# Query weights of the latents: two loads of four heads in place of eight loads of one head

## The chip, the core and the metric

The kernel runs on one core of a Trainium2 chip. The metric is the device time of one execution in microseconds, lower is better. Before the change three runs gave 2002.58, 1998.96 and 2002.11 us, so the median is 2002.11 us. The profiled execution is a run of its own: it took 2000.01 us, of which 1998.2 us are the span from the first to the last instruction.

## The reference, cut to what matters

One layer of a network: a token mixer (state space scan, short convolution, output projection) and then a retrieval stage called PEER. There are 128 context tokens and 512 latent tokens of 1024 values, all float32. The change touches the queries of PEER alone:

```python
PEER_HEADS, PEER_NKEYS, PEER_TOPK, PEER_DQ, TOKEN_BLOCK = 8, 128, 16, 256, 128

def peer(h, w_query, sub_keys, expert_u, expert_v):
    def block(xb):                                   # 128 tokens
        q = (xb @ w_query).reshape(TOKEN_BLOCK, PEER_HEADS, 2, PEER_DQ // 2)
        s = jnp.einsum("thse,sne->thsn", q, sk)
        s1, i1 = lax.top_k(s[:, :, 0], PEER_TOPK)
        s2, i2 = lax.top_k(s[:, :, 1], PEER_TOPK)
        ...
        top, pos = lax.top_k(cand, PEER_TOPK)        # 16 experts for each token and head
        hid = jnp.einsum("thkd,td->thk", expert_u[idx], xb)
        act = gelu(hid) * softmax(top)
        return jnp.einsum("thk,thkd->td", act, expert_v[idx])
```

`w_query` is 1024 x 2048, that is 8 MB; one head's part is 1 MB. Five blocks of 128 tokens with eight heads and sixteen experts make 640 gathers of 128 rows, each row 8 KB (a row of expert_u and one of expert_v side by side).

## The kernel before, in words

The first 230 us or so do the modulation, the scan and the context's mixer. From then on the kernel is one long loop on all engines over G = 0 to 39 (`NALL`), one G for each block of 128 tokens and head: G 0 to 7 are the context's heads, G 8 to 39 those of the four latent blocks. In each G there are eight steps g (`NPR`), and each takes two experts k of the sixteen.

- GpSimd (POOL) issues the gathers, one an expert, into eight slots of 1 MB (`rows`, L1851). Gather k waits until TensorE has used the slot's last content (`v_done`).
- VectorE (DVE) multiplies the gathered rows with the tokens (`dot`, L1654), scales the result (`weigh`, L1663 and L1666), and does in between the top-k of head G+1 (L1595 to L1640).
- ScalarE (ACT) applies the gelu (L1211) and copies scores out of PSUM.
- TensorE (PE) adds the weighted rows (`add_rows`, L841), which frees two slots at each g. It also computes the query of head u = G+2. For the context (u under 8) this is small (L776). For the latents (u = 8 to 15, so G 6 to 13) it is done for all 512 latent tokens at once: `query_lat(u, 0)` stands ahead of `add_rows` at g = 4 and `query_lat(u, 1)` ahead of it at g = 5, 32 matmuls of 128x512 in all (L809), and then come the scores (`scores_lat`, L818) at g = 6. The text calls these 16 us "the block of u". TensorE runs its instructions in order, so in the block `add_rows` comes late, and with it the freeing of slots.
- Beside this, in G 0 to 6, the latents go through their own mixer (`latent_front`): the last output tiles of TensorE (L922, counted by `zol_mm`) are done in G 5, and VectorE normalises the latents (L1737, L1741) in G 6, after which ScalarE modulates them (L1067). Only then can the block of u = 8 start.

SyncE (SP) issues all plain loads, in program order, each behind its wait. There is one place for a head's query weights, `wqb` (r2, 4096 to 6143). `load_query(u)` waits for the last use of that place, which for u = 9 to 15 is the end of the block of u-1, and loads 1024 pieces of 1 KB. After `load_query(12)` the queue holds the first write of results, `y_out` for the context (L467), which waits for `out_ready`. The gathers have a queue of their own (q0); all that SP issues runs in q1. Both share the core's 16 DMA engines.

Two other places matter: `mix_r` from 0 to 5119 holds the mixer's output, which L922 reads; `woA` (r2, 0 to 4095) holds output weights for the same matmuls.

Of the kernel before, what the change touches and what calls it, by code (L numbers as in the profile page):

```python
# [12 lines left out]
P = 128  # L13
D = 1024
KD = D // P
CTX = 128
LAT = 512
T = CTX + LAT
# [4 lines left out]
KS = DS // P  # L23
# [14 lines left out]
HEADS = 8  # L38
TOPK = 16
NKEY = 128  # L40
DQ = 256
# [38 lines left out]
def build(nc, xT, condT, cols, w_mod, w_u, w_tiles, w_o, ssm, bc, dskip, skT, w_query, table, y_out, st_out, kfull):  # L80
    ctx = ExitStack()
    with ctx:
# [6 lines left out]
        bank = [ctx.enter_context(nc.psum_tensor(f"bank{i}", [P, 512], F32)) for i in range(8)]  # L89
# [3 lines left out]
        mix_r = sb("mix_r", [P, KD * T])  # L93
        r1 = sb("r1", [P, 17408])
        r2 = sb("r2", [P, 17408])

        def part(r, a, n):
            return r[:, a:a + n]

        hT = hT_r[:, :].rearrange("p (k t) -> p k t", k=KD)  # L100
# [59 lines left out]
        peer = part(r2, 0, 1024)  # L160
        qTl = part(r2, 1024, 1024).rearrange("p (h t) -> p h t", h=2)
        wqa = part(mix_r, 1024, 2048).rearrange("p (k m) -> p k m", k=KD)
        wqb = part(r2, 4096, 2048).rearrange("p (k m) -> p k m", k=KD)
        h2r = [part(r2, 6144 + 1024 * i, 1024) for i in range(3)] + [part(r1, 16384, 1024)]
        qT = part(r2, 15360, 256).rearrange("p (h t) -> p h t", h=2)
# [71 lines left out]
        ld_wq0 = sem("ld_wq0")  # L237
        ld_wq = sem("ld_wq")
# [59 lines left out]
        yl_mm = sem("yl_mm")  # L298
# [13 lines left out]
        zol_mm = sem("zol_mm")  # L312
# [6 lines left out]
        q_mm = sem("q_mm")  # L319
        q_ev = sem("q_ev")  # L320
        lq_mm = sem("lq_mm")
# [22 lines left out]
        out_ready = sem("out_ready")  # L344
        out_dma = sem("out_dma")
# [11 lines left out]
        NPR = TOPK // 2  # L357
        NALL = NBLK * HEADS
        NQC = 2 * HEADS
# [14 lines left out]
        def _(sp):  # L374
# [55 lines left out]
            sp.dma_start(xtl, xT[:, :, CTX:T]).then_inc(ld_xl, 16)  # L430

            def load_query(u):
                if u == 1:
                    sp.wait_ge(yl_mm, 4)
                elif u <= HEADS:
                    sp.wait_ge(q_mm, u)
                else:
                    sp.wait_ge(lq_mm, 2 * (u - HEADS))
                h = u % HEADS
                sp.dma_start(wqb, w_query[:, :, h * DQ:(h + 1) * DQ]).then_inc(ld_wq, 16)  # L440

            def load_conv_lat(n):
                if n:
# [10 lines left out]
            for n in range(NPR * HEADS):  # L454
                if n in (0, 1, 3):
                    load_conv_lat((n + 1) // 2)
                if 5 <= n < 23 and n % 2:
                    load_conv_lat((n + 1) // 2)
                if n in (34, 35, 36, 37):
                    load_out_lat(n - 30)  # L460
                if n % NPR == 5:
                    load_query(n // NPR + 3)
            for u in range(11, NQC):
                load_query(u)
                if u == 12:
                    sp.wait_ge(out_ready, 1)
                    sp.dma_start(y_out[:, :, 0:P], peer.rearrange("p (k t) -> p k t", k=KD)).then_inc(out_dma, 16)  # L467
            for b in range(1, NBLK - 1):
                sp.wait_ge(out_ready, b + 1)
                sp.dma_start(y_out[:, :, b * P:(b + 1) * P], peer.rearrange("p (k t) -> p k t", k=KD)).then_inc(out_dma, 16)  # L470
# [8 lines left out]
        def _(pe):  # L479
            mm = nc.tensor.matmul  # L480
# [80 lines left out]
            for m in range(KS):  # L561
                for k in range(KD):
                    last = mm(bank[4][:, m * P:(m + 1) * P], wu[:, k, m * P:(m + 1) * P], hT[:, k, 0:CTX], start=(k == 0), stop=(k == KD - 1))
# [234 lines left out]

            def query_lat(u, h):

                if h == 0:
                    pe.wait_ge(ld_wq, 16 * u)
                    pe.wait_ge(sc_ev, u)
                    if u == HEADS:
                        pe.wait_ge(h_ready, 3 * KD - KS)
                else:
                    pe.wait_ge(topk_done, u)
                for k in range(KD):
                    last = mm(bank[2 + h][:, :], wqb[:, k, h * P:(h + 1) * P], hT[:, k, CTX:T], start=(k == 0), stop=(k == KD - 1))  # L809
                last.then_inc(lq_mm, 1)  # L810

            def scores_lat(u):
# [187 lines left out]
            for G in range(NALL):  # L1000
                b, head = G // HEADS, G % HEADS
                t, u = G + 1, G + 2
# [913 lines left out]
```

## Time and profile before

| | |
|---|---|
| median of three runs | 2002.11 us |
| profiled execution | 2000.01 us, span 1998.2 us |
| DVE busy | 1442.3 us, 72% of the span |
| PE busy | 1203.9 us, 60% |
| q0, the gathers | 671.13 MB, 82.3% of 16 engines' span |
| q1, SP's loads and writes | 73.35 MB, 10.4% |
| loads of query weights by SP into r | 15 of 1024 KB |

The page cuts the span in 40 slices of 50 us. The row "GB/s" gives what the DMA engines moved in each: from slice 20 on it stands at 412 to 424 GB/s, which is as much as this kernel ever reaches over such a time, and before that at less. The share of a queue counts the time of its packets against 16 engines over the whole span. Idle time of an engine that is not the bottleneck costs nothing, so the questions to such a page are which engine has no gap in a given stretch, and what the others wait for there.

### The profile page before, as it was taken

The page shows a single profiled execution, that of the slowest core. Times are in us where ns is not written, and L with a number is a line of the kernel's source. Part 1 is how long each engine was busy: PE and PEld are TensorE (multiplying, and loading weights), DVE is VectorE, ACT ScalarE, POOL GpSimd, SP SyncE. Part 2 cuts the span into 40 slices and gives each one's busy share as a digit, 9 for nine tenths or more (in the row PEclk, how much of TensorE's full clock was granted, in tenths as well). Part 3 has the DMA queues.
Part 4 walks back from the last instruction along what each step waited for, and adds up shares of the span by engine and source line. Part 5 has one row for each costly group of instructions (what it writes and reads, how often), then busy time and mean ns, then how long its engine had stood idle before and what let it go on. Part 6 is the DMA issues. An engine that isn't in the chain of part 4 may idle for free.

```text
span 1998.2 us, 24559 instructions
## 1 busy us (share of the span) xinstructions
PE 1203.9 (60%) x8700; PEld 490.3 (25%) x8700; DVE 1442.3 (72%) x3889; ACT 370.2 (19%) x835; POOL 741.5 (37%) x672
## 2 busy tenths in 40 slices
PE   5988888898957766666444443354433445444444
PEld 2558743333413322222111000021000011111001
DVE  8778357787675676767778776777777767877675
ACT  4241242221121221111122101121101112111110
POOL 3100123333333344333443444444444444444442
PEclk8999999999967887777565555566555556556555
DMA  8455489999989999999999999999999999999996
GB/s 335 169 195 198 172 330 373 355 395 389 395 345 378 360 405 401 400 386 387 421 420 420 420 412 414 421 412 410 414 418 421 407 412 414 414 423 412 412 414 259
DMA packets 126107, 746.05 MB, mean 373 GB/s; under 512 B 12112, under 2 KB 34896, under 8 KB 40352
## 3 DMA queue, kind: packets, MB, share of 16 engines
q0 software_dynamic: 92160, 671.13, 82.3%
q1 hardware_dynamic: 33824, 73.35, 10.4%
q8 instruction: 68, 1.11, 0.2%
q14 instruction: 55, 0.45, 0.1%
HBM read 741.78 MB, written 2.65 MB: 373 GB/s over the span
## 4 chain that ended last, share of the span: by engine, by line
DMA 31%; PE 29%; DVE 27%; issue 11%; ACT 2%; POOL 0%; DVEq 0%; POOLq 0%; SPq 0%; ACTq 0%
DMA r<-table,gidx 29%; DVE r L1654 8%; PE bank L841 7%; PE bank L809 6%; PE bank L911 3%; PE bank L922 2%; DMA r<-w_query 1%; DVE wgt L1666 1%; PE bank L858 1%; PE bank L776 1%; DVE r L1622 1%; DVE i L1596 1%; PE bank L537 1%; PE bank L636 1%; DVE i L1602 1%
## 5 line engine op out<-in xcount | busy, mean ns | idle before, releaser
L1851 POOL DMA_INDIRECT r<-table,gidx x640 | 715.5, 1118 | 1198.6 <-PE bank L841 907.9
L1654 DVE CUSTOM_DVE_ANT_0 r<-r 128x1024 f32<-128x1024 f32 x640 | 779.5, 1224 | 305.4 <-DMA r<-table,gidx 282.6
L841 PE MATMUL bank<-r,wgt 128*32 128x512 f32 x2560 | 539.6, 927 | 730.4 <-DVE wgt L1666 704.7
L841 PEld LDWEIGHTS bank<-r,wgt 128*32 128x32 f32 x2560 | 61.7, 130 | 1096.2 <-DVE wgt L1666 1016.1
L1211 ACT ACTIVATE r<-r 128x2 f32<-128x2 f32 x320 | 65.1, 204 | 1045.5 <-DVE r L1654 1036.2
L809 PE MATMUL bank<-hT_r,r 128*128 128x512 f32 x256 | 121.5, 630 | 0.9 <-ACT hT_r L1067 0.9
L1663 DVE TENSOR_TENSOR r<-r 128x2 f32<-128x2 f32 x320 | 49.9, 156 | 90.4 <-ACT r L1211 90.4
L1666 DVE TENSOR_TENSOR wgt<-fold,r 128x64 f32<-128x64 f32 x320 | 72.0, 225 | 11.1
L809 PEld LDWEIGHTS bank<-hT_r,r 128*128 128x128 f32 x256 | 50.3, 202 | 75.2 <-issue 75.2
L1211 ACT ACT_TABLE_LOAD x51 | 65.4, 1283 | 0.9
L858 PE MATMUL bank<-ident,hT_r 128*32 128x128 f32 x1280 | 58.7, 325 | 8.9 <-issue 6.3
L911 PE MATMUL bank<-hT_r,r 128*128 128x512 f32 x128 | 62.1, 630 | 0.0
L922 PE MATMUL bank<-mix_r,r 128*128 128x512 f32 x128 | 60.9, 618 | 0.0
L827 PEld LDWEIGHTS bank<-r,ident 128*32 128x32 f32 x1280 | 44.1, 141 | 54.2 <-DVE r L1633 49.0
L858 PEld LDWEIGHTS bank<-ident,hT_r 128*32 128x32 f32 x1280 | 48.3, 134 | 29.2 <-issue 22.6
L1654 DVE DVE_READ_ACCUMULATOR2_ANT r<- 128x1 f32 x640 | 52.5, 82 | 0.0
L1207 ACT ACT_TABLE_LOAD x40 | 51.3, 1283 | 0.7
L827 PE MATMUL bank<-r,ident 128*32 128x8 f32 x1280 | 47.9, 197 | 3.9 <-DVE r L1633 3.6
L1595 DVE MAX8 r<-r 128x8 f32<-128x128 f32 x80 | 19.3, 283 | 31.0 <-ACT r L1203 16.6
L537 PE MATMUL bank<-hT_r,r 128*128 128x512 f32 x64 | 31.9, 645 | 6.0 <-ACT hT_r L1067 6.0
L1207 ACT ACTIVATE r<-r,small 128x16 f32<-128x16 f32 x40 | 12.3, 308 | 121.8 <-DVE pos L1615 121.7
L911 PEld LDWEIGHTS bank<-hT_r,r 128*128 128x128 f32 x128 | 24.4, 199 | 37.8 <-issue 37.8
(357 smaller groups left out, 1430.4 us busy)
## 6 DMA issues: line engine op xcount, KB each, us to landing
r<-w_mod SPq DMA_DIRECT2D x24, 1024.0 KB, 7.7
r<-w_query SPq DMA_DIRECT2D x15, 1024.0 KB
r<-table,gidx POOLq DMA_INDIRECT x640
r<-w_tiles SPq DMA_DIRECT2D x12, 512.0 KB, 6.5
x_r<-w_tiles SPq DMA_DIRECT2D x10, 512.0 KB, 4.9
hT_r<-xT SPq DMA_DIRECT2D x4, 640.0 KB, 6.3
r<-w_u SPq DMA_DIRECT2D x1, 2048.0 KB, 31.2
r<-w_o SPq DMA_DIRECT2D x1, 2048.0 KB, 10.7
```

The costliest lines, as they stand in the source:

```text
L537: last = mm(bank[m][:, :], wu[:, k, m * P:(m + 1) * P], hT[:, k, CTX:T], start=(k == 0), stop=(k == KD - 1))
L809: last = mm(bank[2 + h][:, :], wqb[:, k, h * P:(h + 1) * P], hT[:, k, CTX:T], start=(k == 0), stop=(k == KD - 1))
L827: last = mm(bank[3][TG * s:TG * s + TG, 8 * tg:8 * tg + 8], ident[:, TG * tg:TG * tg + TG], gi[:, :, 4 * s:4 * s + 4], start=True, stop=True)
L841: last = mm(bank[ACC[b % 2][h]][to:to + TG, :], wgt[:, g % 2, e, :], rows[:, k % SLOTS, D + h * 512:D + (h + 1) * 512], start=(G % HEADS = ...
L858: last = mm(bank[at[k // 4]][TG * s:TG * s + TG, (k % 4) * P:(k % 4 + 1) * P], hT[:, k, t0:t0 + TG], ident[:, :], start=True, stop=True)
L911: last = mm(bank[(4, 5, 7)[r]][:, :], wtl[(tile + 2) % 3][:, k, :], hT[:, k, CTX:T], start=(k == 0), stop=(k == KD - 1))
L922: last = mm(bank[OUT_BANK[m % 3]][:, :], woA[:, m % 4, k, :], mixl[:, k, :], start=(k == 0), stop=(k == KD - 1))
L1207: A(e16, top, ACT.Exp, bias=small[:, 0:1], accum_out=small[:, 1:2]).then_inc(exp_done, 1)
L1211: A(gel[:, par, 2 * g:2 * g + 2], hid[:, par, 2 * g:2 * g + 2], ACT.Gelu_apprx_tanh).then_inc(gelu_done, 1)
L1654: V.tensor_tensor_reduce(rows[:, s, 0:D], rows[:, s, 0:D], h2r[tg], 1.0, 0.0, ALU.mult, ALU.add, hid[:, par, k:k + 1]).then_inc(dot_done, 1)
L1666: tt(wgt[:, g % 2, :, :], fold[:, :].rearrange("p (a m) -> p a m", a=1).broadcast_to([P, 2, TG]), a.rearrange("p (g m) -> p g m", m=1).bro ...
L1851: G_.indirect_dma_start(rows[:, k % SLOTS, :], None, table, bass.IndirectOffsetOnAxis(gidx[:, e, k:k + 1], 0)).then_inc(row_in[k % SLOTS], 16)
```

## The change

The eight loads for the latents, one for each head into `wqb`, become two groups of two loads. Each group brings four heads: one load has the rows k = 0 to 3 of the weights (2 MB, into `mix_r` 0 to 4095), the other the rows 4 to 7 (2 MB, into r2 2048 to 6143, which covers half of `woA` and all of `wqb`). A piece is now 1024 values of one row, 4 KB in place of 1 KB, and there are 512 of them in a load. The bytes are the same, 8 MB.

The first group is issued behind two waits, for the last output tile (`zol_mm`) and for the last use of `wqb` by the context (`q_mm`). The second is issued behind the first write of `y_out` and behind `lq_mm` at 8, the end of the block of u = 11. The matmuls of `query_lat` read another place and wait for another semaphore; their number and shapes stay.

```diff
+        wq4 = [part(mix_r, 0, 4096).rearrange("p (k m) -> p k m", k=KS), part(r2, 2048, 4096).rearrange("p (k m) -> p k m", k=KS)]
...
             def load_query(u):
-                if u == 1:
-                    sp.wait_ge(yl_mm, 4)
-                elif u <= HEADS:
-                    sp.wait_ge(q_mm, u)
-                else:
-                    sp.wait_ge(lq_mm, 2 * (u - HEADS))
-                h = u % HEADS
-                sp.dma_start(wqb, w_query[:, :, h * DQ:(h + 1) * DQ]).then_inc(ld_wq, 16)
+                sp.wait_ge(yl_mm, 4) if u == 1 else sp.wait_ge(q_mm, u)
+                sp.dma_start(wqb, w_query[:, :, u * DQ:(u + 1) * DQ]).then_inc(ld_wq, 16)
+
+            def load_query_lat(n):
+                if n:
+                    sp.wait_ge(lq_mm, HEADS)
+                for part4 in range(2):
+                    sp.dma_start(wq4[part4], w_query[:, KS * part4:KS * part4 + KS, 4 * DQ * n:4 * DQ * (n + 1)]).then_inc(ld_wq0, 16)
...
-                if n % NPR == 5:
+                if n % NPR == 5 and n // NPR + 3 < HEADS:
                     load_query(n // NPR + 3)
-            for u in range(11, NQC):
-                load_query(u)
-                if u == 12:
-                    sp.wait_ge(out_ready, 1)
-                    sp.dma_start(y_out[:, :, 0:P], peer.rearrange("p (k t) -> p k t", k=KD)).then_inc(out_dma, 16)
+                if n == 46:
+                    sp.wait_ge(zol_mm, KD)
+                    sp.wait_ge(q_mm, HEADS)
+                    load_query_lat(0)
+            sp.wait_ge(out_ready, 1)
+            sp.dma_start(y_out[:, :, 0:P], peer.rearrange("p (k t) -> p k t", k=KD)).then_inc(out_dma, 16)
+            load_query_lat(1)
...
             def query_lat(u, h):
 
+                n, at = divmod(u - HEADS, 4)
+                at = at * DQ + h * P
                 if h == 0:
-                    pe.wait_ge(ld_wq, 16 * u)
+                    pe.wait_ge(ld_wq0, 16 + 32 * (n + 1))
...
-                    last = mm(bank[2 + h][:, :], wqb[:, k, h * P:(h + 1) * P], hT[:, k, CTX:T], start=(k == 0), stop=(k == KD - 1))
+                    last = mm(bank[2 + h][:, :], wq4[k // KS][:, k % KS, at:at + P], hT[:, k, CTX:T], start=(k == 0), stop=(k == KD - 1))
```

## Rows read from the trace of the kernel before

**Rows 1.** The page: busy time of the engines, and the gathers' DMA queue.
```profile
PE 1203.9 (60%) x8700; PEld 490.3 (25%) x8700; DVE 1442.3 (72%) x3889; ACT 370.2 (19%) x835; POOL 741.5 (37%) x672
...
q0 software_dynamic: 92160, 671.13, 82.3%
```

**Rows 2.** Stretches: length, busy times, clock share, share of DMA engines, GB/s.
```profile
960.00:1080.00 120.00, 59.43 (x568) 23.59 (x568) 91.93 (x260) 22.86 (x50) 53.22 (x48) 0.60 1.01 420
742.00:771.00 29.00, 12.66 (x95) 3.74 (x93) 23.49 (x72) 5.02 (x12) 13.03 (x12) 0.62 1.01 403
542.00:583.00 41.00, 20.01 (x112) 5.18 (x104) 35.48 (x86) 14.08 (x26) 16.74 (x14) 0.65 0.95 366
```

**Rows 3.** The same view in slices of 1 us, behind two blocks.
```profile
790.00:791.00 1.00, 1.00 (x9) 0.12 (x8) 0.00 (x0) 0.93 (x3) 0.69 (x2) 1.00 0.96 291
...
926.00:927.00 1.00, 1.00 (x10) 0.17 (x9) 0.00 (x0) 0.76 (x3) 0.70 (x2) 1.00 0.00 0
```

**Rows 4.** DMA queues from 789 to 792 us: packets, MB, share of 16 engines.
```profile
q1 hardware_dynamic: 860, 0.87, 93.5%
q0 software_dynamic: 11, 0.06, 12.0%
```

**Rows 5.** DMA queues from 486 to 495 us, during loads of 4 KB pieces (L450).
```profile
q0 software_dynamic: 332, 2.44, 65.2%
q1 hardware_dynamic: 343, 1.27, 35.2%
```

**Rows 6.** TensorE in order of time (start, us): the scores (L818) behind five blocks.
```profile
602.08 2.05 PE L818 MATMUL bank<-sk,r 128*128 128x128 f32 x16
...
787.99 2.05 PE L818 MATMUL bank<-sk,r 128*128 128x128 f32 x16
...
832.71 2.05 PE L818 MATMUL bank<-sk,r 128*128 128x128 f32 x16
...
879.32 2.05 PE L818 MATMUL bank<-sk,r 128*128 128x128 f32 x16
...
924.15 2.05 PE L818 MATMUL bank<-sk,r 128*128 128x128 f32 x16
```

**Rows 7.** VectorE in order of time: the dot of k = 8 behind each of these.
```profile
626.71 1.23 DVE L1654 CUSTOM_DVE_ANT_0 r<-r 128x1024 f32<-128x1024 f32 x1 [0.95 <-DMA r<-table,gidx]
...
812.46 1.23 DVE L1654 CUSTOM_DVE_ANT_0 r<-r 128x1024 f32<-128x1024 f32 x1 [0.66 <-DMA r<-table,gidx]
...
857.90 1.23 DVE L1654 CUSTOM_DVE_ANT_0 r<-r 128x1024 f32<-128x1024 f32 x1 [0.95 <-DMA r<-table,gidx]
...
903.19 1.22 DVE L1654 CUSTOM_DVE_ANT_0 r<-r 128x1024 f32<-128x1024 f32 x1 [0.40 <-DMA r<-table,gidx]
...
947.54 1.21 DVE L1654 CUSTOM_DVE_ANT_0 r<-r 128x1024 f32<-128x1024 f32 x1
```

**Rows 8.** The chain that ended last, from 541 to 584 us.
```profile
543.55 9.32 DMA r<-table,gidx
...
580.50 1.15 DVE r L1654 x2
...
581.88 1.42 ACT hT_r L1067 x2
```

**Rows 9.** The same chain from 741 to 795 us.
```profile
756.92 10.44 DMA r<-table,gidx
...
770.95 8.05 PE bank L809 x16
```

**Rows 10.** VectorE in order of time, G 9.
```profile
722.39 0.17 DVE L1639 COPY r<-bank 128x16 f32<-128x16 f32 x1 [1.12 <-PE bank L827]
```

**Rows 11.** TensorE in order of time: the last output tile of the mixer.
```profile
542.71 3.70 PE L922 MATMUL bank<-mix_r,r 128*128 128x512 f32 x8
```

**Rows 12.** SyncE's queue in order of time around the first write of results.
```profile
741.27 0.61 SPq L467 DMA_DIRECT2D y_out<-r  x1
```

**Rows 13.** The later writes of results (L470), from issue to landing.
```profile
DMA to landing us min/median/max: 23.5/24.2/24.5
```

## Prediction

> **What bounds the kernel now.** I read the page first, then the stretches, then the chain of waits, then the DMA queues in single microseconds. On the page no engine is full, VectorE is busy 72% of the span, but the gathers alone hold 82.3% of the DMA engines over the span [rows 1]. The stretches split this. From 960 to 1080 us, and so on to the end, the DMA share is 1.01 at 420 GB/s [rows 2]: there one gather of 1.05 MB takes 2.5 us, and nothing but bytes counts. The change lies before that, in G 5 to 13 (542 to 924 us). There each G contains the block of u, 16 us in which TensorE frees hardly any slots, so the gathers' queue runs dry at the block's end. The slice 926:927 shows it: DMA share 0.00, 0 GB/s [rows 3]. That block, u = 15, is the only one behind which no query weights are loaded. Behind u = 12, at the same point, the share is 0.96 at 291 GB/s [rows 3], and from 789 to 792 us q1 has 93.5% of the engines and q0 12% [rows 4]. So the eight small loads now run mostly in holes that the blocks leave. That is the reading on which the forecast rests: they cost less than their bytes.
>
> **What goes: small loads behind the blocks.** Loads of u = 9, 10, 11, 13, 14 and 15 have no successor in their places. From the start of the scores (L818) to the dot of k = 8 of the next G there are 24.63 us (602.08 to 626.71), 24.47, 25.19 and 23.87 us behind u = 8, 12, 13 and 14, and 23.39 us behind u = 15, which has no load [rows 6, 7]. The differences are 1.24, 1.08, 1.80 and 0.48 us, sum 4.6 us. In the four first cases the dot waited for a gather (0.95, 0.66, 0.95 and 0.40 us), in the last it did not [rows 7]. The dot of k = 8 matters, since its `weigh` releases the `add_rows` behind which the next block stands. Behind u = 10, in G 9, VectorE waited 1.12 us for TensorE instead [rows 10], so I take 0.4 us there, and nothing behind u = 9, where VectorE has gathers in stock. Gain 5.0 us. Its bounds are six times the smallest and six times the largest difference, 3 and 11 us.
>
> **What comes: the first group, 4.19 MB.** It needs `zol_mm` at 8, and the last tile ends at 542.71 + 3.70 = 546.4 us [rows 11]; the context's queries are done by then. SP has nothing urgent queued behind this wait. In exchange the small load of u = 8, which fell on gather k = 0 of G 6 (9.32 us in the chain from 543.55 us [rows 8]), is gone, and this part becomes up to 2 us shorter. Then the group shares the engines with the gathers. The nearest rows for such sharing are the loads of output weights, also 4 KB a piece: 35.2% for q1, 1.27 MB in 9 us, at 413 GB/s for both queues together ((2.44 + 1.27) / 9) [rows 5]. At 0.14 MB/us, 4.19 MB need 30 us and land near 578 us, ahead of the block of u = 8, which starts when the last modulation ends, at 581.88 + 1.42 = 583.3 [rows 8]. The wait of TensorE costs nothing. But the gathers are later: from 546 us the ten gathers of k = 0 to 9 of G 6 and the group are 10.5 + 4.2 = 14.7 MB, at 420 GB/s 35 us, so k = 9 lands at 581 and its dot starts near 582.5; it now runs at 580.5 [rows 8]. ScalarE modulates the last tiles behind the gelu of this dot. Cost 2 us. The rest of the extra bytes is taken by this stretch itself: from 542 to 583 us DMA moves only 366 GB/s at a share of 0.95, and VectorE is busy for 35.48 of 41 us [rows 2]. Bounds: -2 us, if the stock of landed gathers hides all and only the missing small load counts, and +6 us, if the group stops the gathers of k = 0 to 2.
>
> **The second group, 4.19 MB.** It is issued behind `y_out` at 741.3 us [rows 12], so near 742 us, where the small load of u = 12 was. From 742 to 771 us the DMA share is already 1.01 at 403 GB/s [rows 2], and in the chain the gather of k = 8 takes 10.44 us up to 767.4, from where the block of u = 12 follows at 770.95 [rows 9]. Here nothing hides. 4.19 - 1.05 = 3.15 MB more at 420 GB/s are 7.5 us; less 1.0 us, because the old load moved its 1.05 MB at 291 GB/s (3.6 us) where full rate takes 2.5 us; less what is still missing of the group when k = 8 lands, some 0.2 MB, 0.5 us. Cost 6 us, between 5 and 7.5. The group itself, at 0.14 MB/us after the hole, lands near 775 us, the block would start at 777, so TensorE does not wait.
>
> **The rest.** SP issues four loads in place of eight, which is off every path (it waits most of the time), the matmuls are unchanged in number, form and stride of a column, and from G 14 on nothing differs; a shift at 924 us stays a shift at the end, as all behind it is bound by DMA. Sum: -5.0 + 2 + 6 = +3 us on the profiled 2000.0 us, 2003 us. The median of the runs lies 2.1 us above the profiled execution, so the forecast is 2005 us.
>
> **Rules of the Trainium skill.** "DMA: Bandwidth & Descriptors", Specifications, says that a transfer reaches line rate from 512 B on. By that rule the 1.0 us for slow small pieces falls away, and the sum would be +4, 2006 us; the trace disagrees, with 291 GB/s in a slice whose share is 0.96 [rows 3]. The same page, Queues, rings and completion order, says that an engine takes turns between queues by whole packets of up to 64 descriptors. By that rule a group holds an engine for many pieces at a time; rival (b) is worked out on this.
>
> **Rivals.** (a) *The small loads were dear.* If each costs its full difference at the upper bound (six times 1.8, 11 us) and the first group is hidden (-2), the sum is 11 + 2 - 6 = 7 us faster, 1995. Against it: the hole with 0 GB/s. With milder values, some 3 to 5 us faster. (b) *The groups stop the gathers.* In [rows 4] q0 stood still while a load of q1 ran. If that happens with 64 pieces of 4 KB on each engine, no gather lands for 10 us. For the second group it changes little, the bytes are the same. For the first it delays k = 0 of G 6, and VectorE, busy for most of this stretch [rows 2], cannot catch up: +6 in place of +2, sum +7, 2009 us. Against it: [rows 5], where 4 KB pieces leave q0 65%; and at 546 us two gathers are under way, while at 789 us none was. (c) *TensorE waits for the second group.* It is queued behind `y_out`, and later writes of that size took 24.2 us to land [rows 13]. If on some engine the group starts only at 741 + 24 = 765 us, it lands 10 us (alone) to 30 us (shared) later, 775 to 795. From 777 us on TensorE would stand, free no slots, and the gathers would end: +15 on the sum, 2020 us. It decides once the load lands after 777. Against it: this `y_out` starts in a hole. (d) *The change is hidden altogether*, because the latents' queries are not what G waits for: 2002.
>
> **How the numbers follow.** A measurement of this kernel can tell about 0.2%, 4 us, from no change. Forecast case, +3 (0 to +6): 0.47, of which 0.29 are within 4 us and 0.18 slower. (a) 0.18: faster 0.14, same 0.04. (b) 0.17, slower 0.16, same 0.01. (c) 0.11, slower. (d) 0.07, same. Together faster 0.14, same 0.41, slower 0.45. The range leaves out the upper part of (c) and the outer part of (a): 1997 to 2014; the forecast case alone is 2002 to 2008.
>
> **What would show it.** After the change the time from the scores to the dot of k = 8 should be near 23.4 us behind u = 8, 12, 13 and 14, with DMA near 0 GB/s for 1 to 2 us before; the block of u = 8 should start some 2 us later and that of u = 12 some 6 us later beyond it, less the gain before. No wait of L809 for a load. If q1 holds over 90% of the engines for several us around 548, it is (b); if TensorE stands before L809 in G 10, it is (c). I am wrong at the root if the holes behind the blocks vanish with the loads, since then the small loads made them.

## The result, and the profile after

| | before | after |
|---|---|---|
| median of the runs, us | 2000.94 (1998.96 to 2002.58, 4 runs) | 2013.96 (2011.77 to 2018.14, 4 runs) |
| profiled execution, us | 2000.01, span 1998.2 | 2018.14, span 2016.3 |
| ratio of the times | | 1.0063, 95% interval 1.0046 to 1.0080 |

The changed kernel is slower, by 13 us in the median (one more run of before stands beside it here than above). The profiled execution is the longest of the four, 18 us above that of before. Measured again later (e11 below), against 29 runs of the kernel before with a median of 1992.6 us, it was slower by 6.5 us, 1.0029 (1.0011 to 1.0048). Both intervals lie above 1, and they hardly overlap, so the size is known less well than the sign: weighted by their widths they give about 1.0047, some 9 us, but two results that differ this much leave the mean open by at least half their distance. The traces tell what the two profiled pairs are made of.

First the page of after: the busy times and the gathers' share, which answer to [rows 1]. They are nearly the same; no engine has got clearly more work. (The row "GB/s" of before's page reads 407 to 423 from slice 20 to slice 39, with 259 in the last, and not 412 to 424.)
```profile
PE 1209.2 (60%) x8700; PEld 491.3 (24%) x8700; DVE 1442.5 (72%) x3889; ACT 370.0 (18%) x835; POOL 738.4 (37%) x672
...
q0 software_dynamic: 92160, 671.13, 81.8%
```

Line numbers move by up to five in the changed kernel: the latents' query matmuls are L814, the scores L823, the dot L1659, `add_rows` L846, the group loads L441, the first `y_out` L469. What follows is worked out from the engines' rows in order of time, in six stretches that follow one another and their sum from G 6 on, for the two traces of each pair. G 6 begins with its first dot. The second pair is the repeat (experiments e10 and e11 below).

| stretch, us | before | after | before, again | after, again |
|---|---|---|---|---|
| start of the span to first dot of G 6 | 552.9 | 556.8 | 548.5 | 544.9 |
| to the block of u = 8 | 30.5 | 34.5 | 30.5 | 35.0 |
| to the block of u = 11 | 141.9 | 141.4 | 140.6 | 138.8 |
| to the block of u = 12 | 45.6 | 57.4 | 45.2 | 53.6 |
| to the dot of k = 8 behind u = 15 | 176.7 | 175.8 | 175.4 | 174.1 |
| to the first dot of G 39 | 996.3 | 996.2 | 997.1 | 996.3 |
| first dot of G 6 to that of G 39 | 1391.0 | 1405.2 | 1388.8 | 1397.8 |

Nearly all of the first row lies ahead of anything that the change touches, and it differs by 3.9 us one way and 3.6 us the other. The difference has arisen by the first dot of G 5 (508.6 against 512.6 us, then 504.0 against 500.7). From there to G 6, where the small load of u = 8 is missing in after, all four traces have 44.2 to 44.5 us: that load cost next to nothing, where the forecast allowed up to 2 us. So 4 us of the profiled 18 are no effect of the change. Counted from G 6 on, the change costs 14.2 us in the first pair and 9.0 us in the second. In both the loss sits in two rows, one for each group, and the stretch behind the last block gives nothing back.

The first group. The chain that ended last, in after, up to the block of u = 8 (start, us, what):
```profile
570.08 18.18 DMA r<-table,gidx
588.25 0.02 issue
588.27 1.25 DVE r L1659 x2
...
589.75 1.42 ACT hT_r L1072 x2
591.17 0.14 issue
591.30 1.19 PE bank L814
```
In [rows 8] this place held VectorE's own work; the gather of k = 9 had landed on all 16 engines at 576.0 (the last update of its semaphore), over 4 us before its dot at 580.4. Now it takes 18.18 us to 588.25, and its dot starts at once. Counted by pieces moved, the gathers up to this one were through at 586.0; the other 2.3 us are the wait for the engine that is last. The end of the cover is what the reader should see: a DMA in the chain where VectorE stood.

The second group. TensorE in order of time in after, the scores behind u = 11 and the block of u = 12, and VectorE's dot of k = 8 between them (start, us, what, in brackets the idle time before and what ended it):
```profile
748.78 2.05 PE L823 MATMUL bank<-sk,r 128*128 128x128 f32 x16
```
```profile
782.48 1.23 DVE L1659 CUSTOM_DVE_ANT_0 r<-r 128x1024 f32<-128x1024 f32 x1 [2.37 <-DMA r<-table,gidx]
```
```profile
790.03 5.72 PE L814 MATMUL bank<-hT_r,mix_r 128*128 128x512 f32 x8 [4.00 <-DMA r<-w_query]
```
From the scores to the dot there are 33.69 us; in before it is 25.97 (741.42 to 767.4). That is 7.7 us for the bytes. Then TensorE stands 4.00 us more, and the releaser is the group itself. The chain says since when it was under way; it stands behind `y_out`:
```profile
748.63 0.62 SPq L469
749.25 0.04 issue
749.30 1.37 SPq L441
750.67 0.04 issue
750.71 39.28 DMA r<-w_query
```
And the DMA queues of after from 783 to 790 us (packets, MB, share of 16 engines) show how little was still to come:
```profile
q0 software_dynamic: 399, 2.90, 99.6%
q1 hardware_dynamic: 20, 0.07, 2.4%
```
For 7 us the group crawls with 20 pieces, 2.4% of the engines. From 564 to 574 us, with all 16 engines sharing, a group moved 378 pieces (the row is shown with e4), 2.4 on an engine in a us; 20 pieces in 7 us are thus about what one engine alone moves, or two. Nearly all of the group had landed by 783, and TensorE's wait ends with the last piece.

The packets of q1 and the updates of its semaphores tell why one engine was late. On 15 engines `y_out` was through by 753.7 us; on the last it was through at 761.6. Its pieces have 512 B, and from 756 to 761 us there are still 19 of them (the count under 2 KB less the count under 512 B). In e11, the repeat of after, there is none from 742 to 747 us, as long behind its issue, and it landed 5.9 us after it:
```profile
DMA packets 351, 1.89 MB, mean 379 GB/s; under 512 B 23, under 2 KB 42, under 8 KB 200
```
```profile
DMA packets 346, 1.94 MB, mean 388 GB/s; under 512 B 23, under 2 KB 23, under 8 KB 195
```
Only behind this did the late engine come to its part of the group. The last update of the first load is at 775.7 us, 14.1 us behind the end of `y_out`, and that of the second at 790.0, 14.3 us later; on the 15 other engines the loads ended by 770.9 and 785.0, also some 14 us apart. The trace does not name the engines, but these times fit one engine alone. TensorE was ready at 786.0, so without the late engine it would not have waited.

Behind the blocks the predicted holes are there. Slices of after behind the scores of u = 12 (us, busy times of PE, PEld, DVE, ACT, POOL, clock share, DMA share, GB/s), which answer to [rows 3]:
```profile
809.00:810.00 1.00, 1.00 (x11) 1.00 (x10) 0.57 (x2) 0.00 (x0) 0.97 (x1) 1.00 0.00 0
810.00:811.00 1.00, 1.00 (x10) 0.19 (x9) 0.00 (x0) 0.74 (x2) 0.69 (x2) 1.00 0.00 0
```

### The profile page after: what moved, and what is told of

Read it like the earlier page. It is cut to its first block, busy times and chain, and to the rows that moved or that the text cites. A ratio compares the mean times of both kernels' runs of the same rounds, so it can differ in the third digit from the quotient of the medians.

```text
span 2016.3 us, 24556 instructions
## 1 busy us (share of the span) xinstructions
PE 1209.2 (60%) x8700; PEld 491.3 (24%) x8700; DVE 1442.5 (72%) x3889; ACT 370.0 (18%) x835; POOL 738.4 (37%) x672
## 4 chain that ended last, share of the span: by engine, by line
DMA 32%; PE 30%; DVE 26%; issue 10%; ACT 2%; POOL 0%; DVEq 0%; SPq 0%; POOLq 0%; ACTq 0%
DMA r<-table,gidx 28%; DVE r L1659 8%; PE bank L846 6%; PE bank L814 6%; DMA r<-w_query 3%; PE bank L916 2%; PE bank L927 2%; DVE wgt L1671 1%; PE bank L779 1%; PE bank L863 1%; DVE r L1627 1%; PE bank L540 1%; DVE i L1601 1%; PE bank L639 1%; DVE r L1602 1%
## 5 line engine op out<-in xcount | busy, mean ns | idle before, releaser
L1659 DVE CUSTOM_DVE_ANT_0 r<-r 128x1024 f32<-128x1024 f32 x640 | 779.7, 1224 | 311.0 <-DMA r<-table,gidx 287.4
L846 PE MATMUL bank<-r,wgt 128*32 128x512 f32 x2560 | 541.3, 931 | 739.5 <-DVE wgt L1671 728.9
L846 PEld LDWEIGHTS bank<-r,wgt 128*32 128x32 f32 x2560 | 61.7, 131 | 1105.1 <-DVE wgt L1671 1043.2
L814 PE MATMUL bank<-hT_r,mix_r 128*128 128x512 f32 x128 | 68.2, 682 | 6.0 <-DMA r<-w_query 4.0
L916 PE MATMUL bank<-hT_r,r 128*128 128x512 f32 x128 | 62.7, 635 | 0.0
L814 PE MATMUL bank<-hT_r,r 128*128 128x512 f32 x128 | 57.5, 592 | 0.0
L1659 DVE DVE_READ_ACCUMULATOR2_ANT r<- 128x1 f32 x640 | 52.8, 83 | 0.0
L1600 DVE MAX8 r<-r 128x8 f32<-128x128 f32 x80 | 19.4, 284 | 30.1 <-ACT r L1208 16.7
L814 PEld LDWEIGHTS bank<-hT_r,mix_r 128*128 128x128 f32 x128 | 26.8, 221 | 50.7 <-issue 45.0
L540 PE MATMUL bank<-hT_r,r 128*128 128x512 f32 x64 | 32.1, 649 | 5.9 <-ACT hT_r L1072 5.9
```

Source lines behind the costliest of these rows:

```text
L540: last = mm(bank[m][:, :], wu[:, k, m * P:(m + 1) * P], hT[:, k, CTX:T], start=(k == 0), stop=(k == KD - 1))
L814: last = mm(bank[2 + h][:, :], wq4[k // KS][:, k % KS, at:at + P], hT[:, k, CTX:T], start=(k == 0), stop=(k == KD - 1))
L846: last = mm(bank[ACC[b % 2][h]][to:to + TG, :], wgt[:, g % 2, e, :], rows[:, k % SLOTS, D + h * 512:D + (h + 1) * 512], start=(G % HEADS = ...
L916: last = mm(bank[(4, 5, 7)[r]][:, :], wtl[(tile + 2) % 3][:, k, :], hT[:, k, CTX:T], start=(k == 0), stop=(k == KD - 1))
L1659: V.tensor_tensor_reduce(rows[:, s, 0:D], rows[:, s, 0:D], h2r[tg], 1.0, 0.0, ALU.mult, ALU.add, hid[:, par, k:k + 1]).then_inc(dot_done, 1)
```

## The experiments

All are timed against the kernel before on the chip on which they ran: e1 to e4 on a first one (before 1999.5 us), e5 to e7 on a second (1992.2), e8 to e11 on a third (1992.6), e12 on a fourth (1991.0). The figures with the letter d are the us from the scores of a block to the dot of k = 8 of the next G, as in [rows 6, 7].

**e1, the first group alone.** u = 8 to 11 come from the group, u = 12 to 15 from small loads as before.
```diff
+            load_query(12)
...
-            load_query_lat(1)
+            for u in range(13, NQC):
+                load_query(u)
...
+                    weights = wqb[:, k, h * P:(h + 1) * P] if single else wq4[k // KS][:, k % KS, at:at + P]
```


> Only the first group is loaded as a group (heads of u = 8 to 11); u = 12 to 15 go one by one into wqb as before. Theory A (most of the loss is the second group, which meets gathers that leave DMA no gap): 1 to 4 us over before. Theory B (both groups cost the same, their extra bytes at full rate): 6 to 8 us over before. In the profile the block of u = 8 starts 3 to 6 us later than before, and that of u = 12 no more than that, less 1 to 2 us for the loads of u = 9 and 11 that are gone.


Measured: 2001.68 us, 1.0012 (1.0000 to 1.0023), so 2.4 us slower at best estimate, at the edge of the noise. In its trace the stretch from G 6 to the block of u = 8 has 34.5 us, as in after, and that from u = 11 to u = 12 46.4.

**e2, the second group alone.** u = 9 to 11 are small loads as before, u = 12 to 15 come from the group.
```diff
-                if n == 46:
-                    sp.wait_ge(zol_mm, KD)
-                    sp.wait_ge(q_mm, HEADS)
-                    load_query_lat(0)
+            load_query(11)
```


> Only the second group is loaded as a group (heads of u = 12 to 15); u = 8 to 11 go one by one as before. Theory A: 8 to 12 us over before, with TensorE waiting some 4 us for the load at the block of u = 12. Theory B: 5 to 7 us over before. The two kernels' losses should add up to that of the full change, 13 us, within 3 us.


Measured: 2009.47 us, 1.0046 (1.0030 to 1.0063), 9.3 us slower. G 6 to u = 8 is back at 30.5 us, u = 11 to u = 12 has 54.7, and TensorE does not wait for the load: the loss has the size of theory A, without the wait that belonged to it. The two parts together make 11.7 us; within the noise they add up to the 13 of the full change, and by these two runs four fifths of the loss are the second group's.

**e3, the second group ahead of `y_out`.** The whole change with two statements of SP exchanged.
```diff
+            load_query_lat(1)
             sp.wait_ge(out_ready, 1)
             sp.dma_start(y_out[:, :, 0:P], peer.rearrange("p (k t) -> p k t", k=KD)).then_inc(out_dma, 16)
-            load_query_lat(1)
```


> The full change, with the second group issued ahead of the first write of y_out instead of behind it. Theory C (the write in front of the group on some DMA engine makes it land late): no wait of L809's successor for w_query, 4 to 8 us faster than the full change, some 2007 us. Rival (the load lands late because of its own bytes at a third of the rate): the wait stays, 2012 to 2014 us.


Measured: 2006.83 us, 1.0037 (1.0023 to 1.0052), 7.4 us slower than before. No wait for the load in its trace. The dot and the block of u = 12, VectorE and TensorE in order of time:
```profile
776.48 1.23 DVE L1659 CUSTOM_DVE_ANT_0 r<-r 128x1024 f32<-128x1024 f32 x1 [1.11 <-DMA r<-table,gidx]
```
```profile
779.97 4.70 PE L814 MATMUL bank<-hT_r,mix_r 128*128 128x512 f32 x8
```
The block follows its dot after 3.5 us, as in before, and d is 32.96. With nothing of SP's ahead of the group there is no wait, but the repeat of after (e11) has none either, with the old order. What the exchange is worth in time is not shown by these runs.

**e4, the same bytes in pieces of 1 KB.** Each group is made of eight loads of 0.5 MB.
```diff
-                for part4 in range(2):
-                    sp.dma_start(wq4[part4], w_query[:, KS * part4:KS * part4 + KS, 4 * DQ * n:4 * DQ * (n + 1)]).then_inc(ld_wq0, 16)
+                for i in range(4):
+                    for part4 in range(2):
+                        sp.dma_start(wq4[part4][:, :, DQ * i:DQ * (i + 1)], w_query[:, KS * part4:KS * part4 + KS, DQ * (4 * n + i):DQ * (4 * n + i + 1)]).then_inc(ld_wq0, 16)
```


> The full change with each group cut into eight loads of 1 KB pieces (one head and four rows k each), same bytes at the same places and times. Theory D (an engine with work in both queues takes one piece from each in turn): a 1 KB piece for each 8 KB row of a gather, so a group needs up to 256 turns of 0.35 us, 90 us, TensorE waits for it twice, 40 us or more over before. Rival (an engine takes a whole packet of up to 64 pieces in turn): the group lands as early as with 4 KB pieces or earlier, within 5 us of the full change.


Measured: 2041.94 us, 1.0210 (1.0187 to 1.0233). TensorE's waits from 540 to 1000 us (us in total, times, longest):
```profile
PE bank L815 <- DMA r<-w_query: 38.8, 2, 21.2
```
Its queues from 566 to 574 us, and under them those of after from 564 to 574 us, both with a group and gathers under way:
```profile
q0 software_dynamic: 399, 2.88, 87.1%
q1 hardware_dynamic: 400, 0.40, 15.0%
```
```profile
q0 software_dynamic: 376, 2.72, 64.9%
q1 hardware_dynamic: 378, 1.49, 36.6%
```
399 against 400 packets, 376 against 378: while both queues have work they get the same number of pieces. The late engine of after shows the turns: from 785 to 789.4 us its 4 KB pieces start 0.47 us apart, which is 0.16 us for the piece and 0.31 for one piece of a gather; its 512 B pieces of `y_out` mostly started 0.33 us apart. The gathers' pieces have 8 KB, so a queue with 4 KB pieces gets a third of the bytes and one with 1 KB pieces a ninth. The share of a queue is set by the size of its pieces, and 0.05 MB/us is too little to bring 4.19 MB in time.

**e5, no small loads for the latents.** The kernel before, in which u = 9 to 15 use the weights of u = 8.
```diff
+                if u > HEADS:
+                    return
...
-                    pe.wait_ge(ld_wq, 16 * u)
+                    pe.wait_ge(ld_wq, 16 * min(u, HEADS))
```


> The kernel before without the loads of u = 9 to 15; the blocks of these heads use the weights of u = 8, so 7.3 MB of the 8.4 MB are not loaded and the indices of the gathers differ. This prices the small loads as they stood. Theory A (they run in holes that the blocks leave and only delay the gathers a little): 4 to 7 us faster than before. Theory F (they cost their bytes, 7 times 2.5 us or more): 17 us faster or more. From the scores to the dot of k = 8: 23.4 to 23.9 us behind every block but those of u = 9, 10 and 11.


Measured: 1985.16 us, 0.9966 (0.9947 to 0.9985), 6.8 us faster, for seven loads of 1.05 MB, whose bytes at 420 GB/s [rows 2] take 17.5 us. Its d are 23.40, 23.62, 23.57, 23.82, 23.75, 23.72, 23.40 and 23.40 behind u = 8 to 15. So the small loads did lie mostly in holes; all that there was to be gained by getting rid of all seven, u = 12's among them, was some 7 us. This also answers rival (a), which had put six of them at up to 11 us.

**e6 and e8, small loads half a block earlier.** The kernel before with a second place, in the mixer's output, used in turn; the load of u is released in the middle of the block of u - 1. The two runs are of one kernel.
```diff
-                    sp.wait_ge(lq_mm, 2 * (u - HEADS))
+                    sp.wait_ge(lq_mm, 2 * (u - HEADS) - 1)
...
+                sp.dma_start(wq2 if u > HEADS and u % 2 else wqb, w_query[:, :, h * DQ:(h + 1) * DQ]).then_inc(ld_wq, 16)
```


> The kernel before with two places for a head's weights in turn (wqb and mix_r 0 to 2047), so that each small load of u = 9 to 15 can be issued when the first half of the block of u-1 is done, 7 to 8 us earlier. Theory A (at that point gathers are in stock and TensorE, not DMA, holds the work): most of what leaving them out brings, 3 to 6 us faster than before. Rival (their bytes are merely moved): within 1 us of before.

> The kernel of the two alternating places, once more: the small load of u is issued in the middle of the block of u-1 and so mostly runs while the gathers of the old stock are landing, not behind the block. The first measurement gave -0.8 us with an interval of +-3, while inside its trace the stretch from the start of the block of u=8 to the dot of k=8 of G 15 was 3.6 us shorter (360.5 against 364.1), with the differences 23.40 us behind u=8, 14 and 15. Theory A (the loads behind the blocks cost by their place, the part of the gain that lies in the place): -3 to -4 us, ratio 0.998. Rival (their bytes are paid wherever they lie, and the trace's 3.6 us was chance of one execution): within 1 us of the kernel before.


Measured: e6 1991.55 us, 0.9996 (0.9979 to 1.0013); e8 1989.72, 0.9984 (0.9968 to 1.0000). Together about 0.9990 (0.9978 to 1.0001): 2 us faster at best estimate, and not told apart from no change. The first expectation, 3 to 6 us, was too high. From the block of u = 8 to the dot behind u = 15 the traces have 360.6 and 360.1 us, where the two of before have 364.1 and 361.2. So the 3.6 us that I had read from one pair of traces were in part the scatter of the kernel before.

**e7, half of the second group.** e2 without the second of its two loads; the matmuls of k = 4 to 7 of u = 12 to 15 read what lies there.
```diff
-                for part4 in range(2):
+                for part4 in range(1):
```


> The kernel with only the second group, of which one of the two loads is left out (2.1 MB of 4.2; the rows k = 4 to 7 are whatever lies in that place, so queries of the last four heads are wrong and their gathers' indices differ). Theory G (the group costs its extra bytes at the full rate of 0.42 MB/us): 1.05 MB extra in place of 3.15, so 5 us less than with the whole group, 3 to 6 us over before. Rival (the place or the order in the queue costs, whatever the size): 8 to 10 us over before, as with the whole group.


Measured: 1994.43 us, 1.0010 (0.9991 to 1.0028), 2.2 us slower at best estimate, less than the 3 to 6 expected and not told apart from no change; what follows is read from its trace. u = 11 to u = 12 takes 49.2 us and d is 29.56. So the loss follows the bytes. It is not quite in proportion: 1.05 MB more than before makes the dot 3.6 to 4.0 us later (2.5 at 420 GB/s), 3.15 MB more 7.0 to 8.4 (7.5).

**e9, another pitch of the weights in DRAM.** The whole change; a row of `w_query` has 12 KB in place of 8, so a partition's eight rows have 96 KB in place of 64. The pieces stay 4 KB.
```diff
-    out["w_query"] = a["w_query"][0].reshape(KD, P, -1).transpose(1, 0, 2)
+    out["w_query"] = np.pad(a["w_query"][0].reshape(KD, P, -1).transpose(1, 0, 2), ((0, 0), (0, 0), (0, 1024)))
```


> The whole change, but the rows of w_query in DRAM are 12 KB apart in place of 8 KB; pieces stay 4 KB and bytes are the same. In the traces q1 alone moved only some 300 GB/s, with 1 KB pieces (291) and with 4 KB pieces (0.599 and 0.528 MB in 2 us) alike, where gathers alone move 400 to 420. Theory P (the pitch of 8 KB in DRAM, or a place in DRAM, makes these loads slow): with the other pitch q1 alone moves near 400 GB/s around 750 us, and the second group costs some 1 us less: 1 to 2 us faster than the kernel after. Rival R (the rate belongs to what is read: long pieces one behind another in the direction of SBUF, whatever their pitch): near 300 GB/s again and the time of the kernel after, +11 to +15 us on the kernel before.


Measured: 1997.90 us, 1.0026 (1.0004 to 1.0047), 5.3 us slower and no different from e11's 1.0029 beside it; neither the 1 to 2 us gained nor the +11 to +15 came out. The queue alone, first in e2 from 748 to 751 us with the old pitch, then in e9 from 734 to 736 us:
```profile
DMA packets 266, 0.95 MB, mean 317 GB/s; under 512 B 12, under 2 KB 37, under 8 KB 266
```
```profile
DMA packets 191, 0.77 MB, mean 387 GB/s; under 512 B 1, under 2 KB 2, under 8 KB 191
```
The rate seems better with the new pitch, in one trace of each (in e3, with the old pitch, it was 348 GB/s from 745 to 748 us); the time has nothing of it that these runs can show, and the queue is alone for 2 to 3 us only. The Trainium skill, "DMA: Bandwidth & Descriptors", Latency and other measured facts, has a row on row pitches at large powers of two, where padding by 4 KB gave the full rate back. The pitches that it lists are far larger than the 64 KB here, and e12 speaks against carrying it over to pieces of 1 KB.

**e12, that pitch with the small loads.** The kernel before with the same edit.


> The kernel before, with its small loads, but the rows of w_query in DRAM 12 KB apart in place of 8 KB; pieces stay 1 KB. With that pitch the second group, alone in its queue, moved 0.767 MB in 2 us (384 GB/s) where with 8 KB it had moved 0.599 and 0.528. Theory P (the pitch made all loads of query weights slow, it was not their piece of 1 KB): the small loads alone in their queue move near 380 GB/s behind the block of u=11 to 14, and each dot of k=8 that waited comes 0.5 to 0.8 us earlier, so 2 to 4 us faster than the kernel before. Rival (for 1 KB the piece is the limit, as the forecast had it): near 290 GB/s again, and the time of the kernel before within 1 us. Rival 2 (faster loads gain nothing since the gathers' issue is what is late behind the block): near 380 GB/s, and the time of the kernel before.


Measured: 1989.72 us, 0.9992 (0.9976 to 1.0008). Small loads nearly alone, in e12 from 777 to 779 us and in the repeat of before from 785 to 787 us:
```profile
DMA packets 619, 0.66 MB, mean 329 GB/s; under 512 B 11, under 2 KB 614, under 8 KB 614
```
```profile
DMA packets 609, 0.68 MB, mean 338 GB/s; under 512 B 11, under 2 KB 600, under 8 KB 600
```
The traces show no gain from the pitch for pieces of 1 KB. Why loads of query weights alone stay below the 420 GB/s of the gathers is open.

**e10 and e11, both kernels once more, unchanged.**


> The kernel before, unchanged, with a profile: it shows how far one execution differs from another. Theory N (some 4 us of the profiled 18 are chance, arisen before 541 us, where the two kernels do not differ): G 5 starts anywhere between 499 and 513 us, and from the block of u=8 to the dot of k=8 of G 15 it takes 364 us within 1.5. Rival (the early difference belongs to the changed kernel): G 5 at 508.6 within 1 us again.

> The changed kernel, unchanged, with a second profile beside the second one of the kernel before. Theory N: +11 to +15 us by the median; from the block of u=8 to the dot of k=8 of G 15 374 us within 1.5, the early part as in the other kernels of the same chip, and TensorE waits again 3 to 5 us for the second group. Rival (the wait of TensorE was chance of one execution): no wait for it, and +9 to +10 us.


Measured: e10 1993.47 us in a single run; e11 1999.05 us, 1.0029 (1.0011 to 1.0048), less than the +11 to +15 expected. G 5 starts at 504.0 us in e10 and at 500.7 in e11, against 508.6 and 512.6: the early difference of the first pair was chance. But from the block of u = 8 to the dot behind u = 15 e10 has 361.2 us and before had 364.1, more scatter than the 1.5 us I had allowed. In e11 the dot of k = 8 behind u = 11 and the block of u = 12 are:
```profile
768.84 1.22 DVE L1659 CUSTOM_DVE_ANT_0 r<-r 128x1024 f32<-128x1024 f32 x1 [2.38 <-DMA r<-table,gidx]
```
```profile
772.33 5.12 PE L814 MATMUL bank<-hT_r,mix_r 128*128 128x512 f32 x8
```
No wait for the group. d is 33.96, 8.4 more than in e10. The bytes cost nearly the same as in the first pair, the wait of TensorE did not come again. It is seen in one of five traces with a second group of full size and 4 KB pieces (after, e2, e3, e9, e11). In e2, e9 and e11, as in after, `y_out` stands ahead of the group; there it was through on all engines at 748.7, 734.4 and 740.6 us, 4 to 6 us after its issue, and the group landed 7.1, 6.7 and 2.1 us before the block of u = 12.

## Why the prediction was right and where it was off

The forecast named slower as the likeliest side by a little and 2005 us; the median was 2013.96. Its range, 1997 to 2014, holds this by 0.04 us, which is luck, and its forecast case alone (0 to +6) does not; the +6.5 us of the repeat is just above that case. Rival (d), nothing to be seen, is out by both intervals. Its sum was +2 for the first group, +6 for the second, -5 for the small loads: +3. Counted from G 6 on, the two pairs give +14.2 and +9.0. Term by term:

| term | predicted | first pair | second pair |
|---|---|---|---|
| first group, G 6 to the block of u = 8 | +2 | +4.0 | +4.5 |
| second group, d behind u = 11 | +6 | +7.7 | +8.4 |
| TensorE's wait for it | 0 | +4.1 | 0 |
| d behind the other blocks | -5 | -3.3 | -4.6 |
| elsewhere | 0 | +1.7 | +0.7 |

"Elsewhere" is what remains to the measured sum: the blocks themselves, the us from a dot to the next block, and the end. Where a term was off, it was off to the slow side each time.

**The first group: place and rate right, size off by two.** [rows 5] gave the right share: 0.14 MB/us predicted, 1.49 MB in 10 us measured. By its count of bytes the gather of k = 9 was to be in at 581 and its dot to start at 582.5. Less the 4 us of chance the bytes were in at 582.0 and its dot started at 584.3. Half of the difference is the rate of the stretch, 408 GB/s where the step took 420:
```profile
550.00:587.00 37.00, 13.89 (x89) 3.32 (x87) 32.48 (x77) 12.46 (x21) 13.67 (x12) 0.62 1.01 408
555.00:558.00 3.00, 1.02 (x2) 0.19 (x2) 2.75 (x13) 2.93 (x4) 2.39 (x3) 1.00 1.01 345
```
The other half is the 2.3 us from there to the dot, the wait for the last engine, where I had set 1.5. The group itself landed at 582.6 us, as the step had it (578 and the 4 us), and TensorE did not wait for it. Both rows above have a DMA share of 1.01; the stretch has no more to give, and in before it had 366 GB/s at 0.95 [rows 2]. An underused stretch took 4.2 MB in with a delay of 4 us, in place of the 10 us that the bytes alone take.

**Rival (b) holds for 1 to 2 us.** From 556 to 558 us the gathers' queue is nearly still:
```profile
q1 hardware_dynamic: 140, 0.57, 95.0%
q0 software_dynamic: 12, 0.08, 10.3%
```
That is 9 pieces on each engine, not 64, and 35 KB on each in place of 262. It happens when the gathers' queue has run nearly empty, and it ends late: the next gather was issued at 553.0 us, and q0 moves again from 557.5 on. With q1 idle the first piece of a gather into an empty q0 starts 2.0 us after its issue (behind u = 15 in before), while a small load runs 2.8 to 2.9 us (behind u = 8, 9, 12 and 13). "DMA: Bandwidth & Descriptors", Queues, rings and completion order, of the Trainium skill, lets an engine drain a packet of up to 64 descriptors before it turns; in e4 and after the queues take single pieces in turn (399 against 400, and the steps of 0.47 us on the late engine), and the measurement decides. The other rule of that page of the Trainium skill that was weighed, 512 B for line rate, is not borne out here: pieces of 1 KB nearly alone moved 291 [rows 3], 329 and 338 GB/s, and pieces of 4 KB with the pitch of this kernel 317.

**The second group: the deductions failed.** The bytes are 7.5 us at 420 GB/s, and d grew by 7.7, 8.4, 8.4 (e2) and 7.0 us (e3). I had taken off 1.0 us because the old small load ran at 291 GB/s and put it down to its pieces of 1 KB. Pieces of 4 KB alone in the queue run at 317 GB/s, no better. The bytes that now go through the same hole go at a rate as poor. I had also taken off 0.5 us for what is still missing of the group at the dot. The first 1.05 MB cost more than their bytes (e7), which outweighs this; why is not settled. "Here nothing hides" was right, and the plain 7.5 us would have been the better term.

**Rival (c): the wait came once, by the way it named, its price did not.** By the forecast the group lands at 775 and the block starts at 777. The first `y_out` was issued at 748.63 and not at 741.27 [rows 12], so these become 782.4 and 784.4. On 15 engines the group had landed by 785.0, and TensorE was ready at 786.0: up to there the step holds, with the 1 to 2 us of room that it gave. The last engine had `y_out` until 761.6 and the group until 790.0, 28 us later; rival (c) had said 10 to 30 us for an engine that starts late. So the cause of the wait can be read in this trace, and e3, e2, e9 and e11, in which no engine was held up by `y_out`, have no wait. But TensorE stood 4.0 us, not 15, since nearly the whole group was in. My argument against (c), that `y_out` starts in a hole, holds for three of the four traces that have `y_out` ahead of the group. Why one engine missed the hole in the fourth is not known, nor how many of the executions without a trace had the wait, and so whether it explains part of the step from 6.5 to 13 us.

**The gain: seen where predicted, and partly given back.** d behind u = 8, 12, 13 and 14 is 23.39, 23.75, 23.38 and 23.40 us in after, against 24.63, 24.47, 25.19 and 23.87 [rows 6, 7]; near 23.4 was the forecast. The holes with 0 GB/s are there. In sum the d other than u = 11's fell by 3.3 and 4.6 us, for 5.0 predicted (behind u = 15, where nothing was to change, it grew by 0.5 in the first pair, for a gather). But from the block of u = 12 to the dot behind u = 15, where 3.4 of the 5.0 us were to lie, only 0.9 and 1.3 us are saved. The blocks themselves have become longer, and the granted clock is why. Slices of before in the block of u = 13, which starts at 815.9, and of after, where it starts at 835.4 (the clock share is the third number from the end):
```profile
816.00:817.00 1.00, 1.00 (x4) 0.48 (x3) 0.18 (x2) 0.20 (x1) 0.20 (x1) 0.50 0.98 410
817.00:818.00 1.00, 1.00 (x4) 0.51 (x3) 0.56 (x1) 0.00 (x0) 0.74 (x1) 0.86 0.99 410
818.00:819.00 1.00, 1.00 (x4) 0.52 (x3) 0.97 (x4) 0.00 (x0) 0.95 (x1) 1.00 1.04 434
```
```profile
837.00:838.00 1.00, 1.00 (x2) 0.34 (x1) 1.00 (x1) 0.00 (x0) 0.74 (x1) 0.50 1.03 418
838.00:839.00 1.00, 1.00 (x3) 0.53 (x2) 0.47 (x4) 0.00 (x0) 0.94 (x1) 0.75 0.97 410
839.00:840.00 1.00, 1.00 (x3) 0.38 (x2) 0.56 (x1) 0.00 (x0) 0.00 (x0) 1.00 1.00 418
```
TensorE works through all of them, after a stretch with little work. In before it goes from 1.2 to 2.4 GHz 1.4 us into the block, in after 3.1 us. From the start of a block to its scores the four blocks of u = 12 to 15 take 69.3 and 68.6 us in before, at a mean granted clock of 0.90 to 0.97, and 70.9 and 69.8 in after, at 0.89 to 0.93. The time at which the clock rises differs from block to block within one kernel as well (16.7 to 17.9 us in before), and in e3 and e9, which have the change too, the four blocks take 69.0 and 68.7 us. So I take it as chance of 1 to 2 us and not as an effect of the change. It does limit what a saving of 1 us in one place is worth.

**What is left open:** why `y_out` is late on one engine in some executions, what the first megabyte of a group costs beyond its bytes, and why query weights alone in the queue stay near 320 GB/s (a piece of 4 KB took 0.16 us in turn with gathers, and in the mean 0.20 us with the group alone in e2). The best kernel of the study is neither of the two: small loads released half a block earlier (e6 and e8), by 2 us, if at all.

## What to carry to other kernels

A load that runs mostly in a hole of a busy queue costs well under its bytes (here 1 us in place of 2.5), and it does so because it is small: four times its bytes in one place overflow the hole, and beyond it every megabyte costs what the bottleneck pays, here 2.4 us. Before merging loads ask of each where its bytes will lie, and take the full price of what leaves the hole, without deductions for overheads read from one slice. A load that must be in on time lands with its last engine: look at what stands ahead of it in its queue on each of them. When a delay is a few us in 2000, take two traces of each kernel: here the part of the span that no edit touched differed by 4 us one way and then by over 3 us the other.

## What the runs showed of the hardware

While two queues of an engine both have work they get equal numbers of pieces (399 to 400 with 1 KB pieces, 376 to 378 with 4 KB, against 8 KB of the gathers), so the size of the pieces sets the share of the bytes: 12% and 35%. Cutting the same load into pieces of 1 KB made it land so late that the kernel lost 42 us (e4). Query weights nearly alone on the engines moved 317 to 348 GB/s in stretches of 2 to 3 us, in pieces of 4 KB (317, 348) and of 1 KB (329, 338), where gathers alone moved 420; 4 KB pieces with a row pitch of 12 KB moved 387, in one trace. A load is in when the last of the 16 engines is: one engine that had a write of 0.5 MB until 761.6 us, where the others had it until 753.7, ended the load behind it at 790.0 us in place of 785.0.
